# Three of eight normalised chunks scaled by ScalarE and GpSimd instead of VectorE

## What is computed

```python
def rmsnorm(x, g):
    y = x * lax.rsqrt(jnp.mean(x * x, axis=-1, keepdims=True) + EPS)
    return y * g

for l in range(DEPTH):
    h = rmsnorm(x, norm1_g[l]) * (1.0 + sc1[:, None]) + sh1[:, None]
    x = x + g1[:, None] * token_mixer(h, positions, w_in[l], ret_gn_g[l], sinks[l], w_out[l])
    h = rmsnorm(x, norm2_g[l]) * (1.0 + sc2[:, None]) + sh2[:, None]
    x = x + g2[:, None] * peer(h, peer_wq[l], peer_k1[l], peer_k2[l], peer_u[l], peer_v[l])
return rmsnorm(x, final_g)
```

## Time and profile before

| | us |
|---|---|
| median of 3 runs | 1952.38 |
| lowest and highest run | 1952.11, 1953.32 |
| the profiled execution, its own time | 1955.57 |
| span of its instructions | 1953.7 |
| TensorE busy | 1903.8 (97%) |
| VectorE busy | 1723.0 (88%) |
| ScalarE busy | 1238.1 (63%) |
| GpSimd busy | 498.0 (25%) |

### The profile page before, as it was taken

How to read it: one execution, slowest core, us unless ns; L and a number is a source line. 1 busy time by engine, 2 the same in 40 slices (tenths; PEclk the granted TensorE clock), 3 DMA queues, 4 the chain that set the end, 5 groups by cost and what they waited for, 6 DMA issues and landing times.

```text
span 1953.7 us, 37815 instructions
## 1 busy us (share of the span) xinstructions
PE 1903.8 (97%) x13826; PEld 1832.1 (94%) x13826; DVE 1723.0 (88%) x3225; ACT 1238.1 (63%) x2323; POOL 498.0 (25%) x350
## 2 busy tenths in 40 slices
PE   6999999999999999999999999999999999999998
PEld 6899999999999999999988898999999999999998
DVE  7788888999788899999988978899988888999997
ACT  3478545666899755555455775466669995555554
POOL 0000000000566444455200000000016553545550
PEclk8999999999999999999999999999999999999999
DMA  8776775666565699999867756656665558999994
GB/s 334 244 249 215 260 237 174 205 204 200 202 203 184 237 375 375 370 382 373 316 225 256 251 173 213 227 187 204 203 207 165 170 163 305 378 368 369 367 375 168
DMA packets 139941, 503.73 MB, mean 258 GB/s; under 512 B 16632, under 2 KB 17272, under 8 KB 139304
## 3 DMA queue, kind: packets, MB, share of 16 engines
q1 hardware_dynamic: 115048, 411.95, 61.2%
q0 software_dynamic: 24768, 90.19, 11.8%
HBM read 496.69 MB, written 1.57 MB: 255 GB/s over the span
## 4 chain that ended last, share of the span: by engine, by line
PE 71%; DVE 20%; ACT 5%; issue 3%; DMA 1%; SPq 1%; DVEq 0%; ACTq 0%
PE ps L1893 19%; PE ps L1889 12%; DVE w_lo L919 7%; PE ps L1574 6%; PE ps L1493 6%; PE ps L1489 5%; PE ps L1490 5%; PE ps L1578 3%; PE ps L1486 3%; PE ps L1849 2%; ACT w_hi L596 2%; PE ps L1776 1%; PE ps L1620 1%; DVE hot L1232 1%; DVE hot L1224 1%
## 5 line engine op out<-in xcount | busy, mean ns | idle before, releaser
L596 ACT CAST w_hi<-raw 128x1024 fp32r<-128x1024 f32 x664 | 696.8, 1049 | 658.7 <-PE ps L1889 249.5
L919 DVE TENSOR_TENSOR w_lo<-raw,w_hi 128x1024 fp32r<-128x1024 f32 x664 | 811.0, 1222 | 151.6 <-ACT w_hi L596 147.5
L1574 PE MATMUL ps<-h_both,w_hi 128*128 128x432 f32 x1712 | 373.2, 359 | 0.0
L571 POOL TENSOR_SCALAR hot<-con,rt 128x128 f32<-128x128 f32 x162 | 194.1, 1208 | 622.5 <-DVE neg L1404 518.2
L1574 PEld LDWEIGHTS ps<-h_both,w_hi 128*128 128x128 f32 x1712 | 305.6, 188 | 10.0
L1489 PE MATMUL ps<-h_both,w_hi 128*128 128x256 f32 (+1 forms) x920 | 224.3, 284 | 3.0 <-ACT big L876 2.2
L1578 PEld LDWEIGHTS ps<-h_both,w_lo 128*128 128x128 f32 x1712 | 223.4, 191 | 3.0 <-DVE w_lo L919 0.7
L1578 PE MATMUL ps<-h_both,w_lo 128*128 128x216 f32 x1712 | 224.0, 273 | 0.0
L1490 PE MATMUL ps<-h_both,w_hi 128*128 128x256 f32 (+1 forms) x920 | 220.3, 280 | 0.0
L1893 PE MATMUL ps<-p_both,w_hi 128*128 128x432 f32 x992 | 214.8, 358 | 1.4 <-DVE p_both L1329 1.4
L1893 PE MATMUL ps<-h_both,w_hi 128*128 128x432 f32 x960 | 207.7, 358 | 0.0
(11 more groups left out here) (234 smaller groups left out, 2902.1 us busy)
## 6 DMA issues: line engine op xcount, KB each, us to landing
raw<-in_u SPq DMA_DIRECT2D x256, 512.0 KB, 3.6
raw<-in_v SPq DMA_DIRECT2D x256, 512.0 KB, 6.3
raw<-in_win SPq DMA_DIRECT2D x104, 512.0 KB, 4.4
hot<-in_ada SPq DMA_DIRECT2D x62, 512.0 KB, 4.6
big<-in_ada SPq DMA_DIRECT2D x34, 512.0 KB, 6.7
raw<-in_wq SPq DMA_DIRECT2D x32, 512.0 KB, 4.8
raw<-in_wout SPq DMA_DIRECT2D x16, 512.0 KB, 4.4
big<-in_decay SPq DMA_DIRECT2D x2, 1536.0 KB, 7.9
```

The lines of the kernel that those rows point to most:

```text
L571: last = nc.gpsimd.tensor_scalar(hot2[:, b % 2, t, :], iota, rt[:, 1, col], rt[:, 2, col], ALU.is_equal, ALU.mult)
L596: nc.scalar.copy(w_hi[:, j % 2, :], raw[:, j, :]).then_inc(hi_ready, 1)
L919: tt(w_lo[:, j % 2, :], raw[:, j, :], w_hi[:, j % 2, :].bitcast(F32), ALU.subtract).then_inc(lo_ready, 1)
L1574: mm(o[:, 0:2 * DENSE].rearrange("p (a t) -> p a t", a=2), w_hi[:, s, P * k:P * (k + 1)], h_both[:, :, k, 0:DENSE], start=(k == 0), stop=F ...
```

## The change

In the norms of q = 1, 2 and 3, the scaling of chunks 5, 6 and 7 is split. ScalarE, right behind the root, writes hf = xT * alpha for the three chunks and counts `gained`. GpSimd multiplies each by rstd in place and counts `scaled_pool`; before the first it waits until VectorE has done the scale of chunk 0, by which rstd is known to be there. ScalarE's rounding of these chunks waits for `scaled_pool` instead of `scaled_x`. VectorE leaves the three scales out; its other instructions keep their order. The waits on `scaled_x` count 8 scales for q = 0 and 5 for each of the others.

```diff
+POOL_SCALED = range(5, KC)
...
+            def scales(q):
+
+                pool.wait_ge(scaled_x, KC + POOL_SCALED[0] * (q - 1) + 1)
+                for k in POOL_SCALED:
+                    pool.wait_ge(gained, len(POOL_SCALED) * (q - 1) + k - POOL_SCALED[0] + 1)
+                    nc.gpsimd.tensor_tensor(hf[:, k, :], hf[:, k, :], rs[:, 2, :], ALU.mult).then_inc(scaled_pool, 1)
+
             for l in range(DEPTH):
                 if l:
                     pair_squares(2 * l)
+                    scales(2 * l)
                 pair_squares(2 * l + 1)
+                scales(2 * l + 1)
                 pool.wait_ge(choices_ready, 2 * (l + 1))
...
                 root(q)
+                if q:
+                    for k in POOL_SCALED:
+                        nc.scalar.activation(hf[:, k, :], xT[:, k, :], ACT.Copy, scale=alpha[:, k:k + 1]).then_inc(gained, 1)
                 for k in range(KC):
                     if q == 0 and k % 2 == 0:
                         round_hi(k, k % RING)
-                    act.wait_ge(scaled_x, KC * q + k + 1)
+                    if q and k in POOL_SCALED:
+                        act.wait_ge(scaled_pool, len(POOL_SCALED) * (q - 1) + k - POOL_SCALED[0] + 1)
+                    else:
+                        act.wait_ge(scaled_x, KC * min(q, 1) + POOL_SCALED[0] * max(q - 1, 0) + k + 1)
                     nc.scalar.activation(h_hi[:, k, :], hf[:, k, :], ACT.Identity, bias=mod[:, l, sh + k:sh + k + 1]
...
-                    scale(k).then_inc(scaled_x, 1)
+                    if not q or k not in POOL_SCALED:
+                        scale(k).then_inc(scaled_x, 1)
                     if q == 0 and k % 2:
```

More of the change, by code:

```diff
@@ L380, in build @@
         phi_ready, plo_ready = map(sem, ("phi_ready", "plo_ready"))
-        y_done, y_low, ulow_copied, sq_paired = map(sem, ("y_done", "y_low", "ulow_copied", "sq_paired"))
+        y_done, y_low, ulow_copied, sq_paired, gained, scaled_pool = map(sem, (
+            "y_done", "y_low", "ulow_copied", "sq_paired", "gained", "scaled_pool"))
         ident_ready, picks_ready, picks_spread = map(sem, ("ident_ready", "picks_ready", "picks_spread"))
```

## The result

Over 20 runs each, the changed kernel has a median of 1956.67 us (1954.27 to 1959.60) and the kernel before 1953.10 (lowest 1951.88). The ratio is 1.0015, with a 95% interval of 1.0009 to 1.0021: 2.9 us slower, between 1.8 and 4.1 (the two medians by themselves are 3.6 us apart). Three of all the runs in this study took 3118 to 3734 us, one of the kernel before here among them; they are left out of every ratio and mean. That is less than the 0.2% which the prediction named as what can be told, but clear of noise, and 1956.67 lies above the predicted range, which ended at 1954.6. (The three runs shown ahead of the prediction had a median of 1952.38. Against the 1953.10 of all twenty, the forecast of "nothing" would read 1953.1.)

The account below looks back on a forecast made before the run. TensorE was taken to set the time, except where fed late, as by chunks in norm B. Terms +0.2 (A), +0.2 (C) and -0.4 (B) summed to 0.0 us, median 1952.4 us; range 1950.9 to 1954.6.

Parts of the forecast that it names:

- the forecast of "nothing": Whole kernel: hold-up in part, +0.2 +0.2 -0.4 = 0.0 us over the three norms, median 1952.4; chance 0.40.
- rival (5): ScalarE's new products bring an activation table load in each norm: 2.0 us lost, 1954.4; chance 0.05.
- rival (4): GpSimd starved behind VectorE, products up to 2.9 us each: 8 us lost, 1960.5; decides above 2.0 us; chance 0.04.
- A and C: Norms before the first and second layer's query weights; TensorE behind at half clock; 0.2 us loss taken for each.
- hold-up: GpSimd's product delays a two-input VectorE instruction in the norms, by up to 0.59 us each.
- gain 0: A and C without any hold-up: TensorE is behind until the end, chunk 7 already 0.62 us in hand, nothing gained.
- rival (2): Chunks set the pace in all three norms: 3 x 1.2 = 3.6 us gained, 1948.8; chance 0.03.
- B: Norm between A and C, where chunks set the pace: gain 0.65 us without hold-up, 0.3 with; 0.4 taken.
- Rival (6): Hold-up in full each time: +0.3 us in A and in C, -0.3 in B, 1952.7; chance 0.20.
- Both ends, for A and C: Step bounding A and C: gain 0 without hold-up; in full, chunks 0.8 us late, TensorE reaching chunk 7 0.3 late.
- half-clock stretch: Time in each norm after TensorE's wait when its granted clock is about 0.50 (1.2 of 2.4 GHz), some 3 us.
- rival (3): Late chunk 2 idles TensorE, second half-clock stretch in each norm, 1.5 us lost each: 4.5 us, 1956.9; chance 0.05.

Follow-up runs that it names:

- before_look1: The kernel before, unedited, one further single run with its profile; root to next weight rounding in the three norms added up to 30.21 us.
- dead_scales2: The kernel before, with VectorE doing three further unused scales per norm around chunks 1 and 2, GpSimd untouched; ratio 1.0013 to the kernel before.
- no_product2: The changed kernel without GpSimd's product, so chunks 5 to 7 lack the factor rstd; ratio 0.9999 to the kernel before.

## Why the prediction was wrong

**Right.** ScalarE's three products were costed at nothing, at 1.25 to 1.5 us behind the root; they take 1.29 and are covered, in every run. No table load came: ScalarE has 21 in both kernels, so rival (5) is out. GpSimd was not starved: its products take 0.91 us where 0.73 was assumed, far from the 2.0 from which rival (4) would decide. TensorE set the pace in A and C: without a hold-up their length did not change, so the "gain 0" there was right and rival (2) out. It set it by its clock alone, as the prediction said under that rival: at full clock, without GpSimd's product, A is 8.89 us against 9.46 to 9.67.

**The hold-up was under-weighed.** Its reading from the one long L919 in the earlier trace rows was right, and the Trainium skill's rule (SBUF — State Buffer, "Who interferes with whom"), that a VectorE instruction with two SBUF inputs and a GpSimd instruction that reads SBUF exclude each other, was the better guide than the chance I left for something milder: it happened in every norm, at the instructions named. The sizes: 0.20, 0.47 and 0.46 us, against at most 0.59 each; the low half of chunk 0 late by 0.2 (said: 0.3), chunk 2 by 0.68 (0.8). The page says that the second to issue waits until the first has finished, and this case's traces agree. In norm B the three products end at 995.05, 995.92 and 996.78, which is 0.41, 0.67 and 0.66 us after the starts of the three VectorE instructions, and each is held for 0.2 us less than that. It is so in the other direction too. In before_look1 a sum of squares on GpSimd began at 238.94, with a low half of weights under way on VectorE:

```profile
238.66 1.40 DVE L919 TENSOR_TENSOR w_lo<-raw,w_hi 128x1024 fp32r<-128x1024 f32 x1
...
L557 POOL TENSOR_TENSOR big<-big x12: 727/732/1707, 237.6 to 1940.6; 128x256 f32<-128x256 f32 x12
```

That sum is the one of 1707 ns where 732 is the median: held for 0.98 us, until 0.14 us before L919 ended at 240.06. So the hold-up is what is left of the other engine's instruction, less 0.1 to 0.2 us. Rival (6), the hold-up in full, thus had the hold-up right; its +0.3 us in A and in C was too little, as the next paragraph has it.

**The step that failed** is in "Both ends, for A and C": "TensorE then starts chunk 4 at about 251.4 ..., but that is where the full clock comes back". It took the end of the half-clock stretch as a fixed time, so that work pushed behind it got cheaper, and made 0.8 us of lateness into 0.3, of which the sum then took 0.2. The runs showed two things in its place. At full clock, with no stretch to hide behind, the lateness cost 0.6 us in A and in C (+0.63 and +0.59). And the stretch is not fixed: in ten profiled norms of twelve the granted clock stays at 0.50 for about twice as long as in the kernel before, and over all runs the half-clock time grows by 5.3 us. That is the outcome of rival (3), which was given 0.05, on the ground that 0.8 us is little beside 3.4. It need not be much: dead_scales2, where nothing but the lateness was added, had 4.8 us more. Rival (3) had the second wait as the way to it, which is seen in four of the ten. Its price of 1.5 us a norm was about double what was measured, (33.9 - 30.5 - 1.2) / 3 = 0.7. One reason is that not every norm has the long stretch; another, that part of it falls on time in which TensorE waits anyway. So the sum came out between the forecast and that rival.

**B** was to gain 0.4 us. At full clock it gained 0.13 (10.59 to 10.46), and in the changed kernel as run it lost between 0.2 and 1.1. Without GpSimd's product it gained 1.18, not 0.65. The estimate had TensorE begin chunk 5 at 999.26, because at half clock it was behind until then; in no_product2 the half-clock stretch began with chunk 0 already (its first pair of products took 0.77 us, where it took 0.47 in the kernel before) and so ended sooner, at 996.0 instead of 999.2. At full clock the room in B is 10.59 - 9.30 = 1.3 us, and the hold-up takes 10.46 - 9.30 = 1.16 of it, three times the 0.35 allowed.

**The range** was built from a two-sided view of the hold-up with the clock at one end of it only. Its upper end, +1.3 us, held the 1.1 to 1.3 us that the hold-ups cost at full clock. It did not hold the clock.

## What to carry to other kernels

Before work is handed to GpSimd beside VectorE, look at what both read: two-input VectorE instructions and a GpSimd product take turns, and here 9 products of 0.9 us cost VectorE about as much time as the 9 scales of 0.4 that it was spared, at the place where the chunks were due soonest (3 x 1.13 = 3.4 us against 3.6). And where TensorE came out of a wait of 3.1 to 3.4 us, lateness of the first chunks behind it cost more than itself, as the half-clock time grew too: a gain at the end of such a stage must not be bought with lateness at its start. The clock is best taken out of a comparison by giving TensorE idle products in the long wait; all but one of the stages here then repeated to 0.02 us, and small effects could be seen one by one. And one profile of each kernel is too little where a stretch can be short or long by chance; the mean granted clock of all the runs gives the average.

## What was not expected of the hardware

The same GpSimd form takes 728 ns (sums of squares) and 910 ns as a product beside VectorE, 901 to 916 in all nine. Each of the nine began while a VectorE instruction with two SBUF inputs was under way. The first of them in norm A began 0.16 us after a scale of 0.48 us; what is left of that, less the 0.14 seen with the sum of 1707 ns, is 0.18, and 728 + 180 gives 908. No run has such a product beside an idle VectorE, so this is an estimate. And 24 idle products in the wait kept the granted clock at 1.00 through all three norms in all six profiles where they were put, with later waits of up to 1.19 us in the same norm, while without them the clock fell to 0.50 in every norm of the other twelve profiles, in the tail of the long wait or within 2.1 us behind it.
